# Three v rows of a group added by VectorE, thirteen by TensorE, and a ring of sixteen diagonals

## The chip, the cores and the metric

One core of one Trainium2 chip runs the whole program. The metric is the device time in microseconds. PE is TensorE, DVE VectorE, ACT ScalarE, POOL GpSimd and SP SyncE; each runs its own list of instructions in order, and they wait for one another at semaphores.

## What is computed

An encoder layer over 512 tokens of width 1024: a state-space mixer and latent attention in parallel, a cross-attention to 256 memory tokens, then the expert retrieval with which this document deals, and a last norm. The retrieval, cut to what matters:

```python
def block(xc):                                   # 128 tokens
    q = (xc @ w_q).reshape(T, 8, 2, 128)         # 8 heads, two halves
    s = einsum('thsd,hsnd->thsn', q, sub_keys)
    s1, i1 = top_k(s[:, :, 0], 16);  s2, i2 = top_k(s[:, :, 1], 16)
    cand_s = s1[..., :, None] + s2[..., None, :]
    cand_i = i1[..., :, None] * 128 + i2[..., None, :]
    top_s, pos = top_k(cand_s, 16)
    idx = take_along_axis(cand_i, pos);  gate = softmax(top_s)
    u = take(u_emb, idx, axis=0)                 # rows of 1024 floats
    act = gelu(einsum('thkd,td->thk', u, xc))
    vv = take(v_emb, idx, axis=0)
    return einsum('thk,thkd->td', gate * act, vv)
```

The result is added to the residual stream H, and `rms_norm(H)` is the output. All of it is float32.

## The kernel before

The mixers, the attention and the cross-attention come first; the retrieval begins with the first gather at 767 us. From there the work is cut into 32 groups, numbered g: 8 heads (h), for each the 4 tiles of 128 tokens (t), g = 4h + t. A group needs 16 u rows and 16 v rows for each of its 128 tokens. One gather (line 2003, an indirect DMA that POOL issues) brings one row for each token: 128 rows of 4 KB, so a group has 32 gathers. What each engine does in iteration g:

- POOL (lines 2018 to 2028) issues by turns u row s of group g+1 and v row s of group g, s from 0 to 15. Both have rings of 12 buffers. A u gather waits until the dot product that read its buffer 12 rows ago is done (semaphore `dots`), a v gather until the matmuls that read its buffer 12 rows ago are done (`v_summed`). So v row 12 of group g waits for v row 0 of the same group, and v row 3 of group g for row 7 of group g-1.
- DVE (lines 1473 to 1489) finds the sixteen best keys of group g+2 (`topk`, 25 small steps, each waiting for the one before), takes the finished sum of group g-1 from two PSUM banks into H (`take_sum`, line 1471), makes the 16 dot products of group g+1 (line 1457, one each u row), then, after ACT's gelu, multiplies gelu by gate (`weights`, line 1463, semaphore `w_ready`).
- ACT (lines 943 to 961) copies the queries of head h+1 out of PSUM for t below 2 (line 926), does the exponentials of the gates of group g+2 (930), builds 16 diagonal matrices from the identity and the weights of group g (941), and does the gelu of group g+1 (934). There are 8 diagonal buffers; diagonal s waits until the matmuls of 8 rows ago are done. The gelu stands behind all 16 diagonals in ACT's order.
- PE (lines 1880 to 1885) makes, for t below 2, the queries of head h+1 (line 1854) and the scores from their copy (line 1864), and then sums the group: for each v row, two products of the diagonal with half of the row, 128x512 each, accumulated in two banks (line 1876). The profile has two MATMUL records for each float32 product, so 64 for a group.

After the last group, DVE computes the last norm's variance, ACT its root, and the rows go out.

## Time and profile before

| what | value |
|---|---|
| median of 3 runs | 2350.29 us (2326.3 to 2372.87) |
| the profiled execution | 2343.97 us, span 2342.2 us |
| PE busy | 1807.4 us, 77% |
| DVE busy | 1444.4 us, 62% |
| POOL busy | 1186.4 us, 51% |
| ACT busy | 566.2 us, 24% |
| mean granted clock of PE | 0.896 |
| DMA queue of the gathers | 147840 packets, 537.99 MB, 60.9% of 16 engines' span |

The retrieval takes from 767 us to the end, two thirds of the span. A busy PE there is pipelined matmuls with modelled ends. "Idle before" in the rows below is the time in which the engine did nothing just before such an instruction, with what ended it; "issue" means that the profile shows nothing that it waited for, and "remote" a semaphore whose sender the profile does not name. Every POOL gather has some 0.30 us of idle before it even with nothing to wait for.

### The profile page before, as it was taken

How to read it: one execution, taken by the hardware profiler on the slowest of the kernel's cores; microseconds unless marked ns; L12 is line 12 of the kernel's file. 1: busy time of each engine (PE TensorE's matmuls, PEld its weight loads, DVE VectorE, ACT ScalarE, POOL GpSimd, SP SyncE). 2: the span in 40 equal slices, each digit the busy share in tenths (PEclk: the TensorE clock that was granted, in tenths of full speed). 3: DMA queues.
4: the chain of work that ended last, by engine and by line, in shares of the span. 5: the costliest groups of instructions: out<-in, count | busy, mean ns of one | idle time of the engine just before them, and what ended most of it. 6: DMA issues, size and time to landing. Idle time of an engine off the chain costs nothing.

```text
span 2342.2 us, 19472 instructions
## 1 busy us (share of the span) xinstructions
PE 1807.4 (77%) x6023; PEld 1001.9 (43%) x6023; DVE 1444.4 (62%) x2989; ACT 566.2 (24%) x1201; POOL 1186.4 (51%) x1173
## 2 busy tenths in 40 slices
PE   5978899999998567667777768768857786687587
PEld 5546336779976433223323323323323332232233
DVE  5697773434434566557566676667667666486545
ACT  2344442233333022112111211221211121122111
POOL 6970000000001446765776577667767777667674
PEclk9988999999999778888988889979979898898799
DMA  4303211334323569988999999999999999989997
GB/s 110 63 10 50 68 32 50 95 100 143 126 81 99 190 248 350 367 336 318 387 354 339 343 370 367 379 362 363 382 361 373 365 370 368 346 325 378 349 374 279
DMA packets 243552, 607.27 MB, mean 259 GB/s; under 512 B 38597, under 2 KB 109434, under 8 KB 243450
## 3 DMA queue, kind: packets, MB, share of 16 engines
q0 software_dynamic: 147840, 537.99, 60.9%
q1 hardware_dynamic: 95610, 68.04, 10.4%
q8 instruction: 50, 0.82, 0.1%
q14 instruction: 52, 0.43, 0.1%
HBM read 601.76 MB, written 2.10 MB: 258 GB/s over the span
## 4 chain that ended last, share of the span: by engine, by line
PE 49%; issue 17%; DVE 11%; POOL 9%; another core or an unknown queue 9%; DMA 3%; ACT 2%; SPq 0%; DVEq 0%; ACTq 0%; POOLq 0%
PE bank L1876 26%; PE bank L1565 18%; POOL R L2003 5%; DVE R L991 3%; PE bank L1854 3%; DMA R<-in_peer_v,R 2%; POOL WS L2003 1%; POOL slabs L2003 1%; PE bank L1554 1%; PE bank L1864 1%; DMA XN<-in_x 1%; DVE stat L1249 1%; POOL H L1909 1%; ACT WSr L654 1%
## 5 line engine op out<-in xcount | busy, mean ns | idle before, releaser
L1876 PE MATMUL bank<-R 128*128 128x512 f32 x2048 | 963.9, 629 | 239.4 <-issue 209.4
L1876 PEld LDWEIGHTS bank<-R 128*128 128x128 f32 x2048 | 404.3, 202 | 790.4 <-issue 754.5
L2003 POOL DMA_INDIRECT R<-in_peer_v,R x512 | 525.1, 1026 | 287.7 <-issue 128.8
L941 ACT ACTIVATE R<-cst,R 128x128 f32<-128x128 f32 x512 | 179.7, 393 | 589.4 <-PE bank L1876 327.2
L1999 POOL TENSOR_TENSOR FTr<-slabs,FTr 128x2048 fp32r<-128x2048 f32 x1 | 4.5, 4512 | 542.9 <-ACT FTr L654 542.9
L1457 DVE CUSTOM_DVE_ANT_0 R<-slabs,XN 128x1024 f32<-128x1024 f32 x172 | 210.7, 1225 | 59.8 <-DMA slabs<-in_peer_u,R 33.8
L1457 DVE CUSTOM_DVE_ANT_0 R<-R,XN 128x1024 f32<-128x1024 f32 x168 | 205.7, 1225 | 63.1 <-DMA R<-in_peer_u,R 40.4
L1457 DVE CUSTOM_DVE_ANT_0 R<-WS,XN 128x1024 f32<-128x1024 f32 x172 | 210.7, 1225 | 53.1 <-DMA WS<-in_peer_u,R 32.5
L1565 PE MATMUL bank<-R 128*64 128x64 f32 (+7 forms) x792 | 203.7, 408 | 50.5 <-DVE H L1394 12.8
L2003 POOL DMA_INDIRECT slabs<-in_peer_u,R x172 | 175.1, 1018 | 128.2 <-issue 51.2
L2003 POOL DMA_INDIRECT WS<-in_peer_u,R x172 | 173.3, 1007 | 81.4 <-issue 50.9
L2003 POOL DMA_INDIRECT R<-in_peer_u,R x168 | 169.3, 1008 | 61.7 <-issue 49.7
L1565 PEld LDWEIGHTS bank<-R 128*64 128x64 f32 (+3 forms) x792 | 101.1, 167 | 124.9 <-issue 78.8
L1854 PE MATMUL bank<-FT,slabs 128*128 128x512 f32 (+1 forms) x256 | 118.7, 605 | 31.8 <-issue 25.2
L1864 PE MATMUL bank<-R 128*128 128x128 f32 x120 | 26.5, 390 | 128.1 <-ACT R L926 66.8
L1024 DVE TENSOR_TENSOR WSr<-slabs,WSr 128x1024 fp32r<-128x1024 f32 (+2 forms) x47 | 60.7, 1292 | 103.8 <-ACT WSr L654 103.8
L1471 DVE TENSOR_TENSOR H<-bank,H 128x512 f32<-128x512 f32 x64 | 44.3, 691 | 102.2 <-remote 61.8
L1565 PE MATMUL bank<-Rr,WSr 128*128 128x512 f32 (+1 forms) x448 | 95.4, 366 | 0.0
L991 DVE TENSOR_TENSOR R<-R 128x512 f32<-128x512 f32 (+4 forms) x91 | 76.2, 838 | 27.5 <-POOLq L1987 21.6
L1854 PEld LDWEIGHTS bank<-FT,slabs 128*128 128x128 f32 x256 | 51.8, 205 | 95.5 <-issue 87.7
L926 ACT ACTIVATE R<-bank 128x512 f32<-128x512 f32 (+1 forms) x16 | 9.1, 570 | 319.7 <-remote 286.9
L1565 PEld LDWEIGHTS bank<-Rr,WSr 128*128 128x128 f32 x448 | 77.7, 189 | 13.7
(217 smaller groups left out, 2044.1 us busy)
## 6 DMA issues: line engine op xcount, KB each, us to landing
slabs<-in_w_in SPq DMA_DIRECT2D x17, 512.0 KB, 5.3
slabs<-in_w_mem_kv SPq DMA_DIRECT2D x8, 1024.0 KB, 5.4
slabs<-in_w_peer_q SPq DMA_DIRECT2D x8, 1024.0 KB, 6.7
R<-in_peer_v,R POOLq DMA_INDIRECT x512
slabs<-in_w_in SPq DMA_DIRECT2D x4, 1024.0 KB, 15.0
slabs<-in_w_ssm_glu SPq DMA_DIRECT2D x16, 256.0 KB, 3.1
slabs<-in_w_out SPq DMA_DIRECT2D x4, 1024.0 KB, 5.1
slabs<-in_w_mem_q SPq DMA_DIRECT2D x4, 1024.0 KB, 5.1
```

The lines of the kernel that those rows point to most:

```text
L654: act.activation(hi, src, ACT.Copy).then_inc(w_hi, 1)
L941: act.activation(diag[s % DRING], ident, ACT.Copy, scale=wgt[t % 2][:, s:s + 1]).then_inc(diag_done, 1)
L991: step(dve.tensor_tensor(out, a, b, op))
L1024: dve.tensor_tensor(lo, src, hi, ALU.subtract).then_inc(w_lo, 1)
L1249: step(dve.tensor_reduce(c, b[:, 0:width], AX.X, ALU.max))
L1457: dve.tensor_tensor_reduce(prod, Ub[i % URING], xn[:, t, :], 1.0, 0.0, ALU.mult, ALU.add, act_row[:, s:s + 1]).then_inc(dots, 1)
L1471: lstep(dve.tensor_tensor(h, ps[2 * (t % 2) + n][:, :], h, ALU.add))
L1565: last = pe.matmul(dst, lhs, rhs, start=(n == 0), stop=(n == len(terms) - 1))
L1854: ins = pe.matmul(ps[4 + s][:, cols], qw[:, k, columns(s)], FT[:, k, cols], start=(k == 0), stop=(k == KD - 1))
L1864: ins = pe.matmul(ps[6 + s][:, columns(t)], qhs[s][:, columns(t)], keys, start=True, stop=True)
L1876: last = pe.matmul(ps[2 * (t % 2) + n][:, :], diag[s % DRING], Vb[i % VRING][:, 512 * n:512 * n + 512], start=(s == 0), stop=(s == TOPK - 1))
L2003: pool.indirect_dma_start(out=dst, out_offset=None, in_=table, in_offset=bass.IndirectOffsetOnAxis(ap=ix[:, s:s + 1], axis=0)).then_inc(si ...
```

## The change

- Rows 0, 1 and 2 (`VSLOTS = 3`) of each group leave PE and the diagonals. DVE multiplies each of them by its weight and adds it to H, with one `scalar_tensor_tensor` a row over 128x1024 (`add_rows`), each counted in a new semaphore `v_added`. In DVE's order they stand between the eighth and the ninth dot product.
- A group is 13 rows (`PSLOTS`) for PE and ACT; counts of `diag_done` and `v_summed` are in thirteens.
- A v gather whose buffer held row 0, 1 or 2 waits for `v_added`, the others for `v_summed`.
- There are 16 diagonal buffers; the new eight lie in unused space.
- For t below 2 the scores are issued after the matmuls of v row 8, not ahead of the group.
- In the last group the two roots of ACT stand after all diagonals.

```diff
--- before.py
+++ after.py
@@ -78,7 +78,9 @@
 TOPK_STEPS = 25
 SLAB = 2048
 URING, VRING = 12, 12
-DRING = 8
+VSLOTS = 3
+PSLOTS = TOPK - VSLOTS
+DRING = 16
 
 
 def host_constants():
@@ -311,7 +313,7 @@
         qh2 = reg(0, 2, T)
         SC = reg(1024, NT, 2, NK)
         Vb = [reg(3072 + D * i, D) for i in range(VRING)]
-        diag = [reg(19456 + P * i, P) for i in range(DRING)]
+        diag = [reg((19456 if i < 8 else 1024) + P * i, P) for i in range(DRING)]
         gprow = reg(23040, D)
         gfrow = reg(24064, D)
         prod = reg(25088, D)
@@ -379,6 +381,7 @@
         dots, gelu_done, w_ready, diag_done, v_summed = [
             sem(n) for n in ("dots", "gelu_done", "w_ready", "diag_done", "v_summed")]
         acc_taken, final_done = sem("acc_taken"), sem("final_done")
+        v_added = sem("v_added")
         xg_done = sem("xg_done")
 
 
@@ -933,12 +936,13 @@
                 act.wait_ge(dots, (g + 1) * TOPK)
                 act.activation(gel, act_row, ACT.Gelu_apprx_tanh).then_inc(gelu_done, 1)
 
-            def diagonals(g, t, first=False, slots=range(TOPK)):
+            def diagonals(g, t, slots=range(VSLOTS, TOPK)):
                 act.wait_ge(w_ready, g + 1)
                 for s in slots:
-                    if not first or s >= DRING:
-                        act.wait_ge(v_summed, g * TOPK + (s - DRING + 1))
-                    act.activation(diag[s % DRING], ident, ACT.Copy,
+                    i = g * PSLOTS + s - VSLOTS
+                    if i >= DRING:
+                        act.wait_ge(v_summed, i - DRING + 1)
+                    act.activation(diag[i % DRING], ident, ACT.Copy,
                                    scale=wgt[t % 2][:, s:s + 1]).then_inc(diag_done, 1)
 
             def head(h, first=False, last=False):
@@ -950,12 +954,11 @@
                         gate_exponentials(g + 2)
                     if last and t == NT - 1:
 
-                        diagonals(g, t, slots=range(DRING))
+                        diagonals(g, t)
                         final_root(0)
                         final_root(1)
-                        diagonals(g, t, slots=range(DRING, TOPK))
                     else:
-                        diagonals(g, t, first and t == 0)
+                        diagonals(g, t)
                     if not last or t < NT - 1:
                         gelu_of(g + 1)
 
@@ -1465,11 +1468,20 @@
 
             def take_sum(g, t):
 
-                dve.wait_ge(v_summed, (g + 1) * TOPK)
+                dve.wait_ge(v_summed, (g + 1) * PSLOTS)
                 for n in range(2):
                     h = H[:, t, 512 * n:512 * n + 512]
                     lstep(dve.tensor_tensor(h, ps[2 * (t % 2) + n][:, :], h, ALU.add))
                 dve.sem_inc(acc_taken, 1)
+
+            def add_rows(g, t):
+
+                for s in range(VSLOTS):
+                    i = g * TOPK + s
+                    dve.wait_ge(ld_v[i % VRING], (i // VRING + 1) * 16)
+                    dve.scalar_tensor_tensor(H[:, t, :], Vb[i % VRING], wgt[t % 2][:, s:s + 1], H[:, t, :],
+                                             ALU.mult, ALU.add).then_inc(v_added, 1)
+                    dve.wait_ge(v_added, g * VSLOTS + s + 1)
 
             def head(h, first=False, last=False):
 
@@ -1482,8 +1494,12 @@
                         topk((t + 2) % NT)
                     if not first or t:
                         take_sum(g + (-1), (t - 1) % NT)
-                    if not last or t < NT - 1:
-                        dot_products(g + 1, (t + 1) % NT)
+                    more = not last or t < NT - 1
+                    if more:
+                        dot_products(g + 1, (t + 1) % NT, range(TOPK // 2))
+                    add_rows(g, t)
+                    if more:
+                        dot_products(g + 1, (t + 1) % NT, range(TOPK // 2, TOPK))
                         weights(g + 1, (t + 1) % NT)
                     if ahead:
                         gates_of(g + 2, t)
@@ -1865,24 +1881,27 @@
                 ins.then_inc(s_filled, 1)
 
 
-            def group(g, t, taken=True):
+            def group(g, t, taken=True, then=None):
                 if taken:
                     pe.wait_ge(acc_taken, g - 1)
-                for s in range(TOPK):
+                for s in range(VSLOTS, TOPK):
                     i = g * TOPK + s
+                    n_pe = g * PSLOTS + s - VSLOTS
                     pe.wait_ge(ld_v[i % VRING], (i // VRING + 1) * 16)
-                    pe.wait_ge(diag_done, g * TOPK + (s + 1))
+                    pe.wait_ge(diag_done, n_pe + 1)
                     for n in range(2):
-                        last = pe.matmul(ps[2 * (t % 2) + n][:, :], diag[s % DRING], Vb[i % VRING][:, 512 * n:512 * n + 512],
-                                         start=(s == 0), stop=(s == TOPK - 1))
+                        last = pe.matmul(ps[2 * (t % 2) + n][:, :], diag[n_pe % DRING], Vb[i % VRING][:, 512 * n:512 * n + 512],
+                                         start=(s == VSLOTS), stop=(s == TOPK - 1))
                     last.then_inc(v_summed, 1)
+                    if then and s == TOPK // 2:
+                        scores(*then)
 
             def head(h, first=False, last=False):
                 for t in range(NT):
-                    if t < 2 and not last:
+                    then = (h + 1, t) if t < 2 and not last else None
+                    if then:
                         queries(h + 1, t)
-                        scores(h + 1, t)
-                    group(h * NT + t, t, taken=not first or t >= 2)
+                    group(h * NT + t, t, taken=not first or t >= 2, then=then)
 
             for b in range(8):
                 pe.wait_ge(drained[b], uses[b])
@@ -2012,7 +2031,11 @@
             def v_row(g, t, s):
                 i = g * TOPK + s
                 if i >= VRING:
-                    pool.wait_ge(v_summed, i - (VRING - 1))
+                    was_g, was = divmod(i - VRING, TOPK)
+                    if was < VSLOTS:
+                        pool.wait_ge(v_added, was_g * VSLOTS + was + 1)
+                    else:
+                        pool.wait_ge(v_summed, was_g * PSLOTS + was - VSLOTS + 1)
                 gather(Vb[i % VRING], peer_v, idx[t], s, ld_v[i % VRING])
 
             def head(h, first=False, last=False):
```

POOL's list keeps all gathers in their order; three waits of a group have another semaphore. This is the second half of a group's gathers, before:

```order
L2003 DMA WS<-in_peer_u,R 128x1024 [waits dots]
L2003 DMA R<-in_peer_v,R 128x1024 [waits v_summed]
L2003 DMA WS<-in_peer_u,R 128x1024 [waits dots]
L2003 DMA R<-in_peer_v,R 128x1024 [waits v_summed]
L2003 DMA WS<-in_peer_u,R 128x1024 [waits dots]
L2003 DMA R<-in_peer_v,R 128x1024 [waits v_summed]
L2003 DMA WS<-in_peer_u,R 128x1024 [waits dots]
L2003 DMA R<-in_peer_v,R 128x1024 [waits v_summed]
```

and now (rows 12 to 15 of u and v by turns):

```order
L2022 DMA WS<-in_peer_u,R 128x1024 [waits dots]
L2022 DMA R<-in_peer_v,R 128x1024 [waits v_added]
L2022 DMA WS<-in_peer_u,R 128x1024 [waits dots]
L2022 DMA R<-in_peer_v,R 128x1024 [waits v_added]
L2022 DMA WS<-in_peer_u,R 128x1024 [waits dots]
L2022 DMA R<-in_peer_v,R 128x1024 [waits v_added]
L2022 DMA WS<-in_peer_u,R 128x1024 [waits dots]
L2022 DMA R<-in_peer_v,R 128x1024 [waits v_summed]
```

No gather moved. v rows 12, 13 and 14 of a group now wait for DVE, row 15 for PE.

DVE's list in iteration 9, around the eighth dot product, before (each dot product is a row with a tile and a short row that reads its sum):

```order
L1457 ISA R<-R,XN 128x1024 [waits ld_u10,dots]
L1457 ISA R 128x1
L1457 ISA R<-R,XN 128x1024 [waits ld_u11,dots]
L1457 ISA R 128x1
L1457 ISA R<-slabs,XN 128x1024 [waits ld_u0,dots]
```

and now:

```order
L1460 ISA R<-R,XN 128x1024 [waits ld_u10,dots]
L1460 ISA R 128x1
L1460 ISA R<-R,XN 128x1024 [waits ld_u11,dots]
L1460 ISA R 128x1
L1482 SCALAR_TENSOR_TENSOR H<-R,H 128x1024 [waits ld_v0,dots]
L1482 SCALAR_TENSOR_TENSOR H<-R,H 128x1024 [waits ld_v1,v_added]
L1482 SCALAR_TENSOR_TENSOR H<-R,H 128x1024 [waits ld_v2,v_added]
L1460 ISA R<-slabs,XN 128x1024 [waits ld_u0,v_added]
```

The three adds come behind the u rows that the first eight dot products wait for, and ahead of the other eight.

PE's list over one head, before (x counts products, two for a v row):

```order
L1864 MATMUL bank<-R 128x128 x4
L1876 MATMUL bank<-R 128x512 x96
L1854 MATMUL bank<-FT,slabs 128x512 x8
L1864 MATMUL bank<-R 128x128 x4
L1876 MATMUL bank<-R 128x512 x32
L1854 MATMUL bank<-FT,slabs 128x512 x8
```

and now:

```order
L1870 MATMUL bank<-FT,slabs 128x512 x8
L1893 MATMUL bank<-R 128x512 x12
L1880 MATMUL bank<-R 128x128 x4
L1893 MATMUL bank<-R 128x512 x66
L1870 MATMUL bank<-FT,slabs 128x512 x8
L1893 MATMUL bank<-R 128x512 x12
L1880 MATMUL bank<-R 128x128 x4
L1893 MATMUL bank<-R 128x512 x14
```

A group fell from 32 products to 26, and the scores moved from ahead of it to behind its sixth row.

## Rows read from the trace of the kernel before

**Rows 1.** Stretches: each engine's busy us and count, granted clock, DMA share, GB/s.

```profile
857.00:2332.00 1475.00, 1090.46 (x2376) 468.04 (x2375) 958.27 (x2158) 282.66 (x681) 1001.85 (x984) 0.88 0.94 355
1850.00:1900.00 50.00, 41.39 (x97) 19.11 (x98) 30.43 (x72) 13.46 (x33) 37.29 (x35) 0.87 1.01 387
```

**Rows 2.** Groups of instructions on POOL, 857 to 2332 us: busy, mean ns, idle before.

```profile
L2003 POOL DMA_INDIRECT R<-in_peer_v,R x500 | 512.6, 1025 | 284.0 <-issue 125.1 <-remote 91.1 <-PE bank L1876 67.8
L2003 POOL DMA_INDIRECT WS<-in_peer_u,R x164 | 165.7, 1010 | 79.0 <-issue 48.5 <-DVE R L1457 30.5
L2003 POOL DMA_INDIRECT slabs<-in_peer_u,R x160 | 162.7, 1017 | 54.1 <-issue 48.2 <-DVE R L1457 5.9
L2003 POOL DMA_INDIRECT R<-in_peer_u,R x160 | 160.9, 1006 | 59.3 <-issue 47.2 <-DVE R L1457 12.0
```

**Rows 3.** A wait on POOL, same stretch: us in total, times, longest.

```profile
POOL R L2003 <- remote: 91.1, 49, 4.8
```

**Rows 4.** Groups of instructions on DVE, same stretch, shapes apart.

```profile
L1457 DVE CUSTOM_DVE_ANT_0 R<-WS,XN 128x1024 f32<-128x1024 f32 x168 | 205.8, 1225 | 53.0 <-DMA WS<-in_peer_u,R 32.5 <-DVE R L1457 6.7 <-issue 4.5
L1457 DVE CUSTOM_DVE_ANT_0 R<-slabs,XN 128x1024 f32<-128x1024 f32 x164 | 200.9, 1225 | 59.6 <-DMA slabs<-in_peer_u,R 33.8 <-issue 10.4 <-DVE R L1457 5.0
L1457 DVE CUSTOM_DVE_ANT_0 R<-R,XN 128x1024 f32<-128x1024 f32 x164 | 200.8, 1225 | 63.0 <-DMA R<-in_peer_u,R 40.4 <-issue 6.7 <-DVE R L1457 5.6
...
L1463 DVE TENSOR_TENSOR R<-R 128x16 f32<-128x16 f32 x31 | 5.4, 175 | 69.7 <-issue 46.1 <-ACT R L934 22.5 <-DVE R L1457 1.1
...
L1471 DVE TENSOR_TENSOR H<-bank,H 128x512 f32<-128x512 f32 x62 | 42.9, 691 | 83.6 <-remote 61.8 <-PE bank L1876 12.5 <-DVE R L1444 2.7
...
L1500 DVE SCALAR_TENSOR_TENSOR XN<-H,stat,R 128x1024 f32<-128x1024 f32 x2 | 2.6, 1284 | 0.1
```

**Rows 5.** In order of time, iteration 3: first dot product, u row 12.

```profile
1013.70 1.23 DVE L1457 CUSTOM_DVE_ANT_0 R<-WS,XN 128x1024 f32<-128x1024 f32 x1 [0.19 <-DVE H L1471]
...
1015.20 1.81 POOL L2003 DMA_INDIRECT WS<-in_peer_u,R  x1 [10.63 <-DVE R L1457]
```

**Rows 6.** In order of time, iteration 12: a gather, eighth dot product, v row 12.

```profile
1441.57 0.96 POOL L2003 DMA_INDIRECT R<-in_peer_v,R  x1 [0.30 <-PE bank L1876]
...
1441.75 1.22 DVE L1457 CUSTOM_DVE_ANT_0 R<-R,XN 128x1024 f32<-128x1024 f32 x1
...
1446.63 1.61 POOL L2003 DMA_INDIRECT R<-in_peer_v,R  x1 [0.30 <-issue]
```

**Rows 7.** In order of time, iterations 0 and 30: eighth dot product, v row 12.

```profile
865.75 1.22 DVE L1457 CUSTOM_DVE_ANT_0 R<-R,XN 128x1024 f32<-128x1024 f32 x1
...
866.35 1.45 POOL L2003 DMA_INDIRECT R<-in_peer_v,R  x1 [6.16 <-PE bank L1876]
...
2286.69 0.96 POOL L2003 DMA_INDIRECT R<-in_peer_v,R  x1 [0.30 <-issue]
...
2290.68 1.22 DVE L1457 CUSTOM_DVE_ANT_0 R<-R,XN 128x1024 f32<-128x1024 f32 x1
```

**Rows 8.** POOL in order of time, iteration 8: its v row 12.

```profile
1259.21 1.40 POOL L2003 DMA_INDIRECT R<-in_peer_v,R  x1 [6.21 <-PE bank L1876]
```

**Rows 9.** ACT in order of time, iteration 8: copy, diagonals.

```profile
1252.46 0.60 ACT L926 ACTIVATE R<-bank 128x512 f32<-128x512 f32 x1 [24.05 <-remote]
...
1254.68 2.43 ACT L941 ACTIVATE R<-cst,R 128x128 f32<-128x128 f32 x8
```

**Rows 10.** PE in order of time, iteration 8: scores, then the group.

```profile
1253.11 2.08 PE L1864 MATMUL bank<-R 128*128 128x128 f32 x8 [13.10 <-issue]
1255.21 7.16 PE L1876 MATMUL bank<-R 128*128 128x512 f32 x12
```

**Rows 11.** PE in order of time, one whole group (16).

```profile
1623.34 27.70 PE L1876 MATMUL bank<-R 128*128 128x512 f32 x64 [0.94 <-issue]
```

**Rows 12.** DVE and PE in order of time, the end.

```profile
2302.12 31.12 PE L1876 MATMUL bank<-R 128*128 128x512 f32 x68 [2.36 <-issue]
...
2333.28 1.42 DVE L1471 TENSOR_TENSOR H<-bank,H 128x512 f32<-128x512 f32 x2 [18.59 <-PE bank L1876]
```


## Prediction

> **What bounds the kernel now.** I read the slices of the page first: from a third of the span on, the DMA row stands at 9 while no engine does, and that stretch is the retrieval. So I took the stretch from 857 to 2332 us by itself [rows 1]: POOL busy 1001.85 us for its 984 gathers, DVE 958.27, PE 1090.46 with pipelined records, DMA share 0.94 at 355 GB/s. In its best 50 us the DMA queues moved 387 GB/s at a share of 1.01. A group is 32 gathers of 128 rows of 4 KB, 16.78 MB: 43.4 us at 387 GB/s. The stretch holds 984 / 32 = 30.75 groups, so a group takes 1475 / 30.75 = 48.0 us. The DMA is near its limit, not at it; what is missing are times in which POOL has nothing that it may issue.
>
> POOL is in order, so its list adds up [rows 2]. Busy 1001.85 us, and 0.30 us ahead of each gather even where nothing is waited for, 295 us: 1297 us, or 42.2 a group. The rest is waiting: the v gathers have 284.0 us of idle time ahead of them against 150 for 500 gathers, so 134 are waits for buffers; the u gathers have 79.0 + 54.1 + 59.3 = 192.4 against 145, so 47. "Remote" waits stand only ahead of v gathers, though u and v come by turns; so I read them as `v_summed` that arrived late, like those that name PE. Of these the 49 "remote" ones last 4.8 us at most [rows 3].
>
> DVE is the second loop [rows 4]. A group's 16 dot products have 53.0 + 59.6 + 63.0 = 175.6 us of idle time in all, of which some 0.04 each (20) is normal; 156, or 5.1 a group, is waiting for u rows, so DVE's own round is 48.0 - 5.1 = 42.9 us. In this round stand 69.7 us ahead of `weights` (waiting for the gelu, which stands behind the diagonals) and 83.6 ahead of the take of PE's sum. POOL and DVE are thus both within 6 us of the period, and each waits for the other.
>
> **The change part by part.**
>
> *Adds on DVE.* The nearest instruction is the one of line 1500, the same operation with the same shape: 1.284 us [rows 4], with 0.04 between two as between dot products. Three a group: 4.0 us, 123 us over 30.75 groups. In H and Vb both inputs lie in SBUF, as those of the dot products do, so the v data need nothing more. Below nothing is excluded.
>
> *Where they stand.* u row 12 of the next group may be issued as soon as the first dot product has ended, and POOL does wait for that when DVE is late: in iteration 3 the dot product starts at 1013.70 and POOL has stood for 10.63 us [rows 5]. Now v row 12, POOL's next gather, waits for eight dot products and an add. Take iteration 12: the eighth ends at 1441.75 + 1.22 = 1443.0, the add would be done and seen at 1444.6, and v row 12 was issued at 1446.63 [rows 6]: nothing is lost. In iteration 0 it would be at 865.75 + 1.22 + 1.6 = 868.6 against 866.35, and in iteration 30 at 2293.5 against 2286.69 [rows 7], 6.8 us late. I did this for all 31 iterations: 22 are late, 116 us in sum, the largest 13.2. Two gathers on their way, 43.4 / 32 = 1.36 us each, cover 2.7 us of each, which leaves 62 us. Behind the waiting v row stand u rows 13 to 15, for which DVE waits, and the whole next group.
>
> *Waits that go.* v row 12 waited for PE's first row of the group, as in iteration 8, for 6.21 us [rows 8]; there are nine such waits of over 2 us, 46 us in all, this one the third longest, and they go. The other 88 of the 134 us wait for rows 4 to 15 of the group before. PE now reaches each of these three rows sooner.
>
> *The diagonals and the gelu.* Sixteen buffers for thirteen diagonals: ACT hardly ever waits for PE, and the gelu is free as soon as the dot products are. 69.7 us fall to about 31 x 0.35 = 11: 59 us, or 1.9 a group, off DVE's round. The eight diagonals that are built at once take 2.43 us already [rows 9].
>
> *Scores in mid-group.* They cost 2.08 us of PE, but in iteration 8 they ran from 1253.11 to 1255.19, while ACT went from the copy of the queries at 1252.46 over the exponential to the first diagonals at 1254.68; PE's group starts at 1255.21, a diagonal's 0.4 us after that [rows 9, 10]. So this edit is worth nothing ahead of the group, its cover being ACT; without the cover it would be 2.08 us in 14 groups, 29 us. In mid-group it costs nothing either, while PE isn't the bound.
>
> *PE.* A whole quiet group takes 27.70 us, 0.43 a record, so a v row 1.73 and three rows 5.2 us [rows 11]. That is more than the longest of the 49 waits of [rows 3]. If the signals come by as much sooner, all 88 us go; if they come late for a cause that isn't PE's work, none. Half of the take's 83.6 us should go too, 1.35 us a group: between nothing and 2.7. At the end the last group's 64 records lie bare between 2304 and DVE's take at 2333.28 [rows 12], so there 5.2 us are gained for certain.
>
> *A port rule.* A gather beside a dot product can be as quick as any: 0.96 us at 1441.57, with DVE multiplying from 1441.75 [rows 6]. Over the stretch they average 1.02 [rows 2] against 0.95, so I charge the adds no more than 0.1 us for each of some 90 gathers beside them, 9 us. The Trainium skill (SBUF — State Buffer, Who interferes with whom) says that a VectorE instruction with two SBUF inputs holds off a GpSimd instruction that reads SBUF, the later one fully blocked. If a gather were blocked for each add, 92 x 1.28 = 118 us would be added, by rows and not by a figure of the page; the dot products are such instructions already, and the rows beside them speak against it.
>
> *The sum.* DVE's round becomes 42.9 + 4.0 - 1.9 - 1.35 = 43.6 us where no data is late, POOL's 42.2 plus what it waits. So the period lies between 43.6 and, if the freed time is only waited again at v row 12, 48.0. The shortfall in 22 of 31 iterations says that POOL will wait there often; the 5.1 us that DVE waits for u rows now say that it will arrive earlier when POOL does. I take 46.5, two thirds of the way back: 1.5 x 30.75 = 46 us, and the end's 5, 51. Against this execution's own span 2342.2 that is 2291, and with the 1.8 us around it 2293 to 2294. The execution of these rows, 2343.97, is 6 us under the median of 2350.29, which I leave as noise.
>
> **The rivals.**
>
> *A clear gain, period 43.6.* DVE sets the pace and its round has no more late signals. 4.4 x 30.75 + 5 = 140 us less: 2204. For it: the DMA could do it (43.4). Against it: nothing would be left for jitter between two loops that are chained with no slack.
>
> *Nothing much moves.* The signals that come late are late because the DMA queues are full, not because PE has much to do. A fuller queue then makes as much waiting as was freed. For it: 61.8 us of DVE's waits for PE's sum end "remote" [rows 4], like POOL's. Period 47.5: 15 + 5 less, 2324.
>
> *Slower, through v row 12.* One mechanism: POOL waits for DVE's eight dot products and the add, with none of the 88 us freed. 62 + 9 - 5 = 66 more: 2410. It decides from the point where the waits at v row 12 pass 2 us a group more than what is freed elsewhere. For it: 22 of 31. Against it: the gelu's 1.9 us and the take's bring DVE there sooner, which pays for most of the adds.
>
> *The blocked gathers* of the rule above would end at 2294 + 118 = 2412 as well; I give them 2 in 100, within the 21 of the slower case. That the change does not do what it says I leave out: the order of the instructions shows it.
>
> **How the numbers follow.** Forecast (2260 to 2325) 0.42, clear gain 0.12, nothing much 0.25, slower 0.21. Two per cent, about what a measurement of this kernel can tell from no change, is 2303 and 2397 against the median. Faster: the clear gain, 0.27 of the forecast's 0.42, 0.02 of the third: 0.41. Slower: two thirds of the last, 0.14. The rest 0.45. The range from 2230 to 2390 leaves out most of the clear gain and half of the slower case.
>
> **What would show it.** Right: PE's group at 22 to 23 us in quiet stretches; idle time ahead of `weights` near 11 us in all; adds of 1.28 us, 96 of them; waits of POOL on v gathers that have moved from PE and "remote" to DVE's line of the adds, and are fewer than 134 us; a DMA share over 0.94. Wrong: POOL's waits on the adds over 110 us with "remote" waits as before (slower); a share of 1.0 (clear gain); gathers with a mean well above 1.02 (the port); DVE's small steps stretched further (nothing much).

## The result, and the profile after

The changed kernel takes **2448.66 us**, median of 5 runs (2424.37 to 2490.98), against 2350.29 before (2326.3 to 2372.87): ratio 1.0438, 95% interval 1.0379 to 1.0497. It is slower by over 4%, above the predicted range of 2230 to 2390. The profiled execution is the longest of the five, 42 us above their median and in a slower state than three of them, so its rows show the loss too large, and the main waits are read from variants of the changed kernel as well.

The page of after, and the retrieval's stretch of both kernels (columns as in [rows 1]):

```profile
span 2489.2 us, 18701 instructions
...
PE 1690.8 (68%) x5639; PEld 928.6 (37%) x5639; DVE 1568.1 (63%) x3085; ACT 511.0 (21%) x1105; POOL 1194.8 (48%) x1173
...
q0 software_dynamic: 147840, 537.99, 56.9%
...
DVE 30%; issue 23%; PE 21%; POOL 11%; DMA 7%; another core or an unknown queue 5%; ACT 1%; SPq 1%; DVEq 0%; ACTq 0%; POOLq 0%
...
857.00:2480.00 1623.00, 972.13 (x1988) 392.75 (x1986) 1079.25 (x2253) 227.77 (x585) 1009.46 (x984) 0.81 0.85 323
```

Against [rows 1] POOL is busy for the same 1000 us in 984 gathers, but in 1623 us instead of 1475, and the DMA share fell from 0.94 to 0.85. Nothing became more expensive; POOL stands still for longer. The groups of POOL and its waits, and DVE's lines, in the same stretch of after:

```profile
L2022 POOL DMA_INDIRECT R<-in_peer_v,R x500 | 518.7, 1037 | 363.5 <-DVE H L1482 185.9 <-issue 139.6 <-remote 30.6
L2022 POOL DMA_INDIRECT WS<-in_peer_u,R x164 | 166.8, 1017 | 93.0 <-issue 52.0 <-DVE R L1460 40.9
L2022 POOL DMA_INDIRECT slabs<-in_peer_u,R x160 | 163.4, 1021 | 78.3 <-issue 47.6 <-DVE R L1460 30.8
L2022 POOL DMA_INDIRECT R<-in_peer_u,R x160 | 161.5, 1009 | 84.5 <-issue 46.9 <-DVE R L1460 37.6
...
POOL R L2022 <- DVE H L1482: 185.9, 24, 10.1
POOL R L2022 <- PE bank L1893: 7.4, 13, 2.5
...
L1482 DVE SCALAR_TENSOR_TENSOR H<-R,H 128x1024 f32<-128x1024 f32 x96 | 123.4, 1285 | 7.1 <-DVE R L1460 1.7 <-issue 1.6
L1474 DVE TENSOR_TENSOR H<-bank,H 128x512 f32<-128x512 f32 x63 | 43.6, 692 | 86.4 <-PE bank L1893 32.5 <-remote 23.6 <-DVE R L1447 13.3
L1466 DVE TENSOR_TENSOR R<-R 128x16 f32<-128x16 f32 x31 | 5.4, 175 | 13.6 <-issue 5.8 <-ACT R L937 3.9 <-DVE R L1460 2.1
```

Ahead of the v gathers stand 363.5 us, where [rows 2] had 284.0, and 185.9 of them are 24 waits for an add. The waits on PE fell from 67.8 to 7.4 and the "remote" ones from 91.1 to 30.6. Ahead of the u gathers DVE's dot product now ends 109.3 us of waiting, where [rows 2] had 48.4. So both of POOL's links to DVE grew, by 247 us, and the others lost 121. Two variants that come further below, with shorter profiled executions, show the same waits for an add: 179.2 us in 24 with half rows, 151.4 in 22 with the diagonals first.

One round in order of time. First POOL, whose gathers from 1603.64 to 1632.02 follow one another with no wait:

```profile
1601.06 0.95 POOL L2022 DMA_INDIRECT R<-in_peer_v,R  x1 [0.31 <-remote]
...
1631.07 0.95 POOL L2022 DMA_INDIRECT slabs<-in_peer_u,R  x1 [0.30 <-issue]
1634.47 0.94 POOL L2022 DMA_INDIRECT R<-in_peer_v,R  x1 [2.46 <-PE bank L1893]
1637.34 1.81 POOL L2022 DMA_INDIRECT WS<-in_peer_u,R  x1 [1.93 <-DVE R L1460]
1647.53 1.87 POOL L2022 DMA_INDIRECT R<-in_peer_v,R  x1 [8.38 <-DVE H L1482]
```

Then PE and DVE, same round:

```profile
1606.31 1.98 PE L1893 MATMUL bank<-R 128*128 128x512 f32 x4 [1.19 <-DMA R<-in_peer_v,R]
1618.04 7.29 PE L1893 MATMUL bank<-R 128*128 128x512 f32 x12 [9.74 <-DMA R<-in_peer_v,R]
...
1616.97 0.18 DVE L1447 SCALAR_TENSOR_TENSOR R<-R 128x16 uint32<-128x16 f32 x1
1634.24 1.42 DVE L1474 TENSOR_TENSOR H<-bank,H 128x512 f32<-128x512 f32 x2 [17.09 <-PE bank L1893]
1635.84 1.23 DVE L1460 CUSTOM_DVE_ANT_0 R<-WS,XN 128x1024 f32<-128x1024 f32 x1 [0.19 <-DVE H L1474]
...
1645.98 3.93 DVE L1482 SCALAR_TENSOR_TENSOR H<-R,H 128x1024 f32<-128x1024 f32 x3
```

The two pieces together tell the price. u row 12 (1637.34) had to wait for the first dot product, and v row 12, the very next gather, waited 8.38 us for the add, since eight dot products and an add take from 1635.84 to 1647.3. Of the 24 waits 17 are of 8.38 or 8.39 us: whenever POOL has caught up with DVE at u row 12, it pays the whole of it. Meanwhile the DMA queues run empty (columns as in [rows 1]; the last two are their share and GB/s):

```profile
1640.00:1644.00 4.00, 1.30 (x4) 0.23 (x2) 3.90 (x7) 0.00 (x0) 0.00 (x0) 1.00 0.39 122
1644.00:1648.00 4.00, 0.00 (x0) 0.00 (x0) 3.89 (x6) 0.00 (x0) 0.47 (x1) 0.72 0.00 0
```

The other thing to see is why DVE was late here: it stood for 17.09 us before the take. The take of this group waits for PE's last row of it, and that is the record at 1606.31, ended by 1608.3 (all 32 x 52 records of the groups are in the trace, and by their count the rows from 1618.04 on are the next group's, whose diagonals ACT built at 1614.37). Its signal was seen 26 us later, by DVE at 1634.24 and by POOL at 1634.47 alike. I had read such waits as short ones.

The waits and the key search in both traces. "Loop" is the time from the first dot product of group 1 to the last one; the waits are POOL's beyond 0.30 us a gather; the last column adds up DVE's gaps of over 0.5 us ahead of the small steps of the key search in the loop.

| kernel | loop | at u row 12 | v rows 12 to 14 | other v | key search |
|---|---|---|---|---|---|
| before | 1444 | 45 | 46 | 88 | 132 |
| after | 1592 | 108 | 180 | 34 | 249 |

After's waits at v rows 12 to 14 are +134 us, at u row 12 +63, at the other v rows -54; together 143 of the 148 us of the longer loop.

### The profile page after: what moved, and what is told of

Read it like the earlier page. It is cut to its first block, busy times and chain, and to the rows that moved or that the text cites. A ratio compares the mean times of both kernels' runs of the same rounds, so it can differ in the third digit from the quotient of the medians.

```text
span 2489.2 us, 18701 instructions
## 1 busy us (share of the span) xinstructions
PE 1690.8 (68%) x5639; PEld 928.6 (37%) x5639; DVE 1568.1 (63%) x3085; ACT 511.0 (21%) x1105; POOL 1194.8 (48%) x1173
## 4 chain that ended last, share of the span: by engine, by line
DVE 30%; issue 23%; PE 21%; POOL 11%; DMA 7%; another core or an unknown queue 5%; ACT 1%; SPq 1%; DVEq 0%; ACTq 0%; POOLq 0%
PE bank L1581 18%; POOL R L2022 7%; DVE R L1460 4%; DVE R L994 3%; PE bank L1893 2%; DVE H L1474 2%; DMA WS<-in_peer_u,R 2%; DMA slabs<-in_peer_u,R 2%; DVE H L1482 2%; DVE R L1413 2%; DVE R L1414 2%; DMA R<-in_peer_u,R 2%; DVE R L1415 2%; DVE R L1417 1%
## 5 line engine op out<-in xcount | busy, mean ns | idle before, releaser
L1893 PE MATMUL bank<-R 128*128 128x512 f32 x1664 | 866.8, 671 | 643.7 <-issue 278.5
L1893 PEld LDWEIGHTS bank<-R 128*128 128x128 f32 x1664 | 338.0, 213 | 1161.6 <-issue 808.7
L2022 POOL DMA_INDIRECT R<-in_peer_v,R x512 | 531.2, 1037 | 367.2 <-DVE H L1482 185.9
L937 ACT ACTIVATE R<-R 128x16 f32<-128x16 f32 x32 | 6.9, 216 | 834.7 <-issue 465.4
L1482 DVE SCALAR_TENSOR_TENSOR H<-R,H 128x1024 f32<-128x1024 f32 x96 | 123.4, 1285 | 7.1 <-DVE R L1460 1.7
L1027 DVE TENSOR_TENSOR WSr<-slabs,WSr 128x1024 fp32r<-128x1024 f32 (+2 forms) x47 | 60.7, 1292 | 103.9 <-ACT WSr L657 103.9
L945 ACT ACTIVATE R<-cst,R 128x128 f32<-128x128 f32 x416 | 124.6, 386 | 2.2 <-remote 1.5
L1474 DVE TENSOR_TENSOR H<-bank,H 128x512 f32<-128x512 f32 x64 | 44.3, 692 | 86.4 <-PE bank L1893 32.5
```

The costliest lines, as they stand in the source:

```text
L945: act.activation(diag[i % DRING], ident, ACT.Copy, scale=wgt[t % 2][:, s:s + 1]).then_inc(diag_done, 1)
L1027: dve.tensor_tensor(lo, src, hi, ALU.subtract).then_inc(w_lo, 1)
L1474: lstep(dve.tensor_tensor(h, ps[2 * (t % 2) + n][:, :], h, ALU.add))
L1482: dve.scalar_tensor_tensor(H[:, t, :], Vb[i % VRING], wgt[t % 2][:, s:s + 1], H[:, t, :], ALU.mult, ALU.add).then_inc(v_added, 1)
L1893: last = pe.matmul(ps[2 * (t % 2) + n][:, :], diag[n_pe % DRING], Vb[i % VRING][:, 512 * n:512 * n + 512], start=(s == VSLOTS), stop=(s == ...
L2022: pool.indirect_dma_start(out=dst, out_offset=None, in_=table, in_offset=bass.IndirectOffsetOnAxis(ap=ix[:, s:s + 1], axis=0)).then_inc(si ...
```

## The experiments

Runs of one group shared a core and its runs of the kernel before. All ratios are to these.

**First group: the parts one by one** (before 2349.08 us). Theory O at this point: the order, POOL waiting at v row 12 for DVE's middle, costs the time. Rival L: DVE's load of 4 us an iteration does.

The wait alone, in the kernel before:

```diff
                 if i >= VRING:
                     pool.wait_ge(v_summed, i - (VRING - 1))
+                if s == 12 and g + 1 < NG:
+                    pool.wait_ge(dots, (g + 1) * TOPK + 9)
                 gather(Vb[i % VRING], peer_v, idx[t], s, ld_v[i % VRING])
```

> The kernel before, in which v row 12 of each group also waits for the ninth dot product of the next group, about the moment at which the first add would be done. No add is made. Theory O (the order: POOL's list stands still at v row 12 while the DMA queues run dry): most of the 98 us come back, 2420 to 2450 us, with waits of some 8 us at that gather. Theory L (load: the 4.0 us of adds in each of DVE's rounds make the time): under 2370 us.

Measured: 2418.39, ratio 1.0268 (1.0207 to 1.0329), just under the range of theory O. POOL's waits at v rows 12 to 14 are 135 us (before 46), those at the other v rows fell from 88 to 29, and POOL's gathers themselves took 38 us more in the loop (1026 against 988), which no edit here explains:

```profile
L2003 POOL DMA_INDIRECT R<-in_peer_v,R x500 | 537.4, 1075 | 314.1 <-issue 136.0 <-DVE R L1457 77.9 <-PE bank L1876 76.9
```

The load alone, in the kernel before, is three operations of the same form into a scratch tile, between the eighth and ninth dot product:

```diff
-                        dot_products(g + 1, (t + 1) % NT)
+                        dot_products(g + 1, (t + 1) % NT, range(TOPK // 2))
+                        for s in range(3):
+                            lstep(dve.scalar_tensor_tensor(prod, xn[:, (t + 1) % NT, :], wgt[t % 2][:, s:s + 1],
+                                                           xn[:, (t + 1) % NT, :], ALU.mult, ALU.add))
+                        dot_products(g + 1, (t + 1) % NT, range(TOPK // 2, TOPK))
```

> The kernel before, in which DVE makes three operations of the adds' form and shape (into a scratch tile, so they change no result) between the eighth and the ninth dot product of each iteration but the last. PE still sums all sixteen rows. Theory O: 31 x 4.0 = 124 us of DVE work hide mostly behind waiting for u rows, 2350 to 2385 us. Theory L: 2420 us or more.

Measured: 2346.33, ratio 1.0016 (0.9963 to 1.0069). The load costs nothing there that can be told from zero. L falls.

The changed kernel with `VSLOTS = 0`, so that ring, scores and split remain:

> The changed kernel with no row on DVE (VSLOTS = 0): what is left is the ring of sixteen diagonals and the scores in mid-group. Both theories: the idle time ahead of the weights falls from 70 us to about 11, so 2300 to 2345 us. If it is over 2380 us, the loss is in the diagonals or the scores, and both theories fall.

Measured: 2339.07, ratio 0.9943 (0.9904 to 0.9981). The wait for the gelu went as predicted (its line has 11.3 us of idle time ahead, where [rows 4] had 69.7), but ahead of the take the idle time rose (these rows hold all 64 instructions of the take, the last group's too, for which before has 102.2 us and not the 83.6 of [rows 4] with 62):

```profile
L1474 DVE TENSOR_TENSOR H<-bank,H 128x512 f32<-128x512 f32 x64 | 44.2, 691 | 124.0 <-remote 60.5 <-PE bank L1893 55.8 <-issue 2.0
L1466 DVE TENSOR_TENSOR R<-R 128x16 f32<-128x16 f32 x31 | 5.4, 176 | 11.3 <-issue 6.0 <-ACT R L937 3.9 <-DVE R L1460 1.4
```

So of the 58 us freed at the gelu 22 came back as waiting for PE's sum, and the gain is 0.6%.

The changed kernel with `add_rows` ahead of all dot products, so that v row 12 waits for DVE's first work after the take:

> The changed kernel with the three adds ahead of all sixteen dot products. v rows 12 to 14 are then free before u row 12 is, so POOL's one wait is that for the first dot product, 4.0 us later than before. Theory O: 2330 to 2390 us, and no wait of some 8 us at v row 12. Theory L: as the changed kernel, 2430 to 2460 us.

Measured: 2508.88, ratio 1.0664 (1.0594 to 1.0733), a clear miss. POOL's waits at v rows 12 to 14 went to zero, and those at u row 12 to 280 us:

```profile
POOL slabs L2020 <- DVE R L1460: 108.2, 10, 21.9
POOL WS L2020 <- DVE R L1460: 104.7, 9, 21.3
POOL R L2020 <- DVE R L1460: 96.9, 8, 14.8
```

The order of the adds is thus not the point. Whatever stands ahead of a dot product for which POOL waits is paid, and DVE was later than before by more than the adds: its key search had 419 us of gaps.

**Second group: without a wait for the adds** (before 2326.88). Theory C: POOL's wait for the chain take, first dot product, later ones is what is paid, and load ahead of the first dot product costs too. Rows 4, 5 and 6 instead of 0, 1 and 2 on DVE; their buffers are wanted again only by v rows 0, 1 and 2 of the next group, so POOL has no wait for the adds in mid-group (the start of the edit):

```diff
-VSLOTS = 3
+VSLOTS, VLO = 3, 4
+ON_PE = [s for s in range(TOPK) if not VLO <= s < VLO + VSLOTS]
```

> The changed kernel with rows 4, 5 and 6 of each group on DVE in place of 0, 1 and 2; the adds stand where they stood, behind the eighth dot product. The buffers that they free are wanted by v rows 0 to 2 of the next group, some 9 us after v row 12. v row 12 waits for PE's first row again. Theory O (POOL's wait at v row 12 in mid-group is the loss, DVE's adds themselves are free there): 2310 to 2360 us, like the kernel with no adds. If the loss is the coupling of POOL to DVE's adds wherever it is: 2400 us or more.

Measured: 2423.36, ratio 1.0348 (1.0257 to 1.0438). POOL waits 10 us at v rows 12 to 14 and 222 at u row 12. Another miss: taking the wait away moved it. What also grew is DVE's key search, 372 us of gaps against 132. Why POOL should wait so much longer for the first dot product here than with the load alone, whose DVE work has the same place (222 us against 80), no run tells. One such stretch of this kernel, POOL and DVE:

```profile
2004.20 0.95 POOL L2025 DMA_INDIRECT R<-in_peer_v,R  x1 [0.30 <-issue]
...
1991.56 0.09 DVE L1418 MATCH_VALUE_LOAD R<-R 128x8 f32 x1 [1.09 <-DVE R L1417]
1993.67 0.29 DVE L1419 MAX8 R<-R 128x8 f32<-128x128 f32 x1 [1.76 <-issue]
1995.06 0.09 DVE L1420 MATCH_VALUE_LOAD R<-R 128x8 f32 x1 [1.09 <-issue]
1997.86 0.18 DVE L1435 CAST R<-R 128x32 f32<-128x32 uint32 x1 [2.44 <-remote]
1999.27 0.42 DVE L1436 TENSOR_TENSOR R<-R 128x256 f32<-128x256 f32 x1 [1.23 <-issue]
2000.66 0.43 DVE L1416 MAX8 R<-R 128x8 f32<-128x256 f32 x1 [0.97 <-DVE R L1436]
2002.06 0.09 DVE L1417 MATCH_VALUE_LOAD R<-R 128x8 f32 x1 [0.97 <-DVE R L1416]
2004.16 0.09 DVE L1418 MATCH_VALUE_LOAD R<-R 128x8 f32 x1 [1.60 <-issue]
2006.96 0.43 DVE L1419 MAX8 R<-R 128x8 f32<-128x256 f32 x1 [2.31 <-remote]
...
2009.87 0.17 DVE L1442 TENSOR_SCALAR R<-R 128x16 uint32<-128x16 uint32 x1 [0.66 <-DVE R L1440]
```

Each step waits for nothing but the one before on DVE itself, and starts 1.40, 2.10 or 2.80 us after it, multiples of 0.70; in after's round above most of the same steps start within 0.04 us of the end of the one before. PE stood idle here from 1982.4 to 2010.65. The last late step starts at 2009.87, some 5 us after POOL's last gather, which ended at 2005.15.

The three extra operations in the kernel before, ahead of all dot products:

> The kernel before, in which DVE makes three operations of the adds' form and shape into a scratch tile ahead of its sixteen dot products, not amid them. No row leaves PE, no v buffer waits for DVE. The kernel with the adds first took 2509 us. Theory C (what sets the time is DVE's chain from its small steps to the first dot product, for which u row 12 and so POOL waits; time amid the dot products is free): 2450 to 2520 us. If the adds' position costs only through v buffers: 2350 to 2380 us.

Measured: 2436.67, ratio 1.0499 (1.0447 to 1.0552), though DVE's load is that of the kernel that lost nothing. The 3.9 us an iteration stand between the take and the first dot product: 31 x 3.9 = 121 us, of which 110 arrive.

Theory S is that full DMA queues stretch DVE's small steps. Half gathers, of 64 partitions, after the first twelve (the other partitions keep old rows, so the sums are not the layer's):

> The kernel before with the same half gathers (output not the reference's). Theory S: the time from the weights to the take falls from 18 us to 12 to 14, PE's late signals go (no diagonal waits much over 1.3 us for a row), 2080 to 2200 us, and the changed kernel with half gathers is within 2 per cent of it. If the changed kernel stays 4 per cent behind, its loss doesn't need full queues.

> The changed kernel with only 64 of 128 rows in each gather after the first twelve u and v gathers; the other partitions keep what is there, so the output is not the reference's. POOL has as many gathers, the DMA queues half the bytes. Theory S (DVE's small steps stretch, from about 12 to over 20 us a group, because the DMA queues are full beside them): the time from the weights to the take falls to 12 to 14 us, and the kernel to 2100 to 2250 us, with a few us of wait at v row 12 left. If the stretching has another cause, it stays at 20 us or more.

Measured: 2326.16, ratio 0.9995 (0.9957 to 1.0032), and 2357.55 from two runs (2338.89 and 2376.22), too few for an interval. I can't use them as meant: the bytes halved (275.84 MB), but the queues stayed busy for 51.8% of the span; a packet took longer. As far as two runs go, the changed kernel lies 31 us, 1.3%, behind here and not 4.4%, although it waits 106 us at v rows 12 to 14 (29 without the change): at u row 12 it waits 18 us and not 92. So a wait at v row 12 isn't lost in every case; why this pair loses less is open.

**Third group: a shorter chain in the key search** (before 2339.65). Theory R: signals travel late, so each of the 25 small steps that waits for the one before costs. The ten steps of the first stage run on two halves by turns, each waiting for the last but one:

```diff
-                for s in range(2):
-                    top16(SC[:, t, s, :], sc1, tv[:, s, :], ti[:, s, :])
+                for k in range(5):
+                    for s in range(2):
+                        ...
+                        lstep([lambda: dve.max(v[:, 0:8], vals),
...
+                               lambda: dve.max_index(ix[:, 8:16], v[:, 8:16], spare)][k](), lag)
```

> The kernel before with its key search in pairs: the five steps on the one half of the keys and the five on the other by turns, each waiting only for its own predecessor, and two more steps that don't wait for the one before. Same instructions, ten fewer waits in a row. Theory R (the stretched time of DVE's small steps is the round trip of each step's own semaphore, at the place that sets the first dot product): 4 to 6 us a group less from the weights to the take, and 2260 to 2320 us. If the steps are late for another reason, the time stays within 1 per cent of before.

> The changed kernel without adds (ring of sixteen, scores in mid-group) and the search in pairs. Theory R: the shortest round of DVE of all four, and so the fastest: 2230 to 2300 us, which would beat both kernels. If R is wrong, about 2339 us as without pairs.

> The changed kernel with the same search in pairs. Theory R: its period is DVE's round, so nearly the whole gain arrives: 31 x 4 to 6 us, 2270 to 2350 us. Otherwise 2430 us or more.

> Rows 4, 5 and 6 on DVE, and the search in pairs. Theory R: DVE's round of 52 us falls to 46 to 48, so 2260 to 2320 us. If R is wrong, 2400 us or more.

Measured, in this order: 2338.61, ratio 1.0002 (0.996 to 1.0043); 2334.96, 0.9957 (0.991 to 1.0003); 2418.19, 1.0282 (1.0197 to 1.0367); 2389.8, 1.0179 (1.0088 to 1.0271). On before and on the kernel without adds it gives nothing; on after 1.0438 becomes 1.0282 and on rows 4 to 6 1.0348 becomes 1.0179, each against its own core's before. That speaks for DVE's round as what sets the pace in the kernels with adds and not in before. It doesn't show it: the intervals of after's pair all but touch (from 1.0379 and to 1.0367), those of rows 4 to 6 overlap (from 1.0257 and to 1.0271), and neither pair stood on one core. The expected times (2270 to 2350 and 2260 to 2320 us) were missed by far.

**Fourth group: full queues, or not?** (before 2326.12). A rival to POOL's issuing as the cause of the late signals was that the DMA queues are full. Half rows on all 128 partitions, after the first twelve gathers (the right halves keep old data):

> The kernel before with gathers of 128 rows of 2 KB (half a row) after the first twelve u and v gathers; the right halves keep old data, so the output is not the reference's. Theory S (late updates need full queues): the key search is not stretched (12 to 14 us from the weights to the take), PE's signals come in time, and the time is 2100 to 2230 us. If the lateness comes from the gathers' count and not from their bytes: as before within 2 per cent, with the key search at 18 us or more.

> The changed kernel with the same gathers of half rows (output not the reference's). Theory S: 2130 to 2280 us, the key search not stretched, v row 12's wait still there. Otherwise: 2380 us or more.

Measured: 2299.28, ratio 0.9844 (0.9767 to 0.9922), and 2414.17 from two runs. The traffic of the first in the stretch:

```profile
857.00:2290.00 1433.00, 1079.66 (x2351) 464.70 (x2349) 951.41 (x2149) 276.23 (x667) 994.04 (x982) 0.88 0.64 185
...
q0 software_dynamic: 83840, 275.84, 41.5%
```

The queues are busy 0.64 of the time instead of 0.94, at half the GB/s, and the key search still has 145 us of gaps (before 132), POOL's waits at other v rows are 84 (88). So the lateness doesn't need full queues. And with half the bytes after loses as much, 2414 against 2299, with 172 us of waits at v rows 12 to 14. Its key search has 108 us of gaps, fewer than the 145 of the kernel before with half rows: the loss doesn't need a key search more stretched than before's.

The diagonals ahead of the exponentials in ACT's order, so that PE starts without waiting for the key search:

> The changed kernel without adds (ring of sixteen, scores in mid-group), with ACT building a group's diagonals ahead of the exponential of the gates of two groups later. PE may then start a group when its weights are ready, some 20 us sooner. Theory P (PE's late start, tied to DVE's key search, makes POOL's waits ahead of v rows, 134 us in the kernel before): 2220 to 2300 us, and most of these waits gone. If POOL's waits move to the u rows instead: 2320 to 2345 us.

> The changed kernel with its adds, diagonals first. Its waits at v row 12 are for DVE's adds and not for PE. Theory O: they stay, some 8 us each, and the time stays at 2400 to 2450 us. If PE's late start had a part in the loss: under 2390 us.

Measured: the kernel without adds 2330.37, ratio 1.0024 (0.998 to 1.0069), the changed one 2427.6, 1.0343 (1.0239 to 1.0446). Ahead of the take the idle time fell to 64.3 us in the first, from 124.0 in the kernel without adds of the first group, and the kernel was no faster: POOL's waits at u row 12 became 105 us instead of 54, those at v rows 12 to 14 fell from 50 to 8. An earlier PE is not worth anything here.

**Fifth group, on another chip** (before **2170.24**, 2168.25 to 2171.75 in 13 runs). The kernel before itself runs 7% faster there. Two kernels ran: wait and load together in the kernel before (here the wait is for eight dot products, some 1.3 us sooner than for the nine of the wait alone), and rows 4 to 6 with a pause of eight small operations on POOL, ahead of u row 6 in each iteration:

> The kernel before with both: v row 12 waits for the eighth dot product of the next group (1.3 us sooner than the add), and DVE makes three operations of the adds' form into a scratch tile behind that dot product. Sixteen rows on PE, eight diagonals, the scores ahead of the group. If the change is these two and nothing else: 2420 to 2460 us, the changed kernel's loss. If the two only add up as measured alone (2.7 and 0 per cent): 2385 to 2405 us.

> The kernel with rows 4, 5 and 6 on DVE (2423 us, 3.5 per cent behind), in which POOL makes eight fills of an unused tile, some 5 us, ahead of u row 6 of each group, that is in the midst of the gathers that run beside DVE's key search. Theory U (an unbroken run of gathers makes DVE's updates late): the search gets shorter by more than a little (rest of DVE's round under 24 us, now 25.7) and the time is the same or up to 2 per cent less, 2340 to 2420 us. If the lateness has nothing to do with the run: POOL's spare time takes the pause at best and the time is the same or more, with the same search.

Measured: wait and load 2169.89, ratio **0.9999** (0.9989 to 1.0008); the pause 2340.72, 1.0773 (1.0745 to 1.08). Their rows, the first three of wait and load, the last of the pause:

```profile
857.00:2100.00 1243.00, 1010.08 (x2223) 412.74 (x2221) 1028.02 (x2180) 267.33 (x638) 948.68 (x944) 0.95 1.02 404
...
L2007 POOL DMA_INDIRECT R<-in_peer_v,R x497 | 495.4, 997 | 158.3 <-issue 133.5 <-PE bank L1880 19.9 <-DVE R L1457 4.9
...
L1471 DVE TENSOR_TENSOR H<-bank,H 128x512 f32<-128x512 f32 x64 | 44.2, 691 | 27.0 <-PE bank L1880 21.3 <-DVE R L1444 0.5
```

```profile
L2054 POOL MEMSET R<- 128x600 f32 x248 | 148.9, 601 | 12.6
```

No "remote" wait, no gap of over 0.5 us in the key search of the loop (132 us in before on its chip), a DMA share of 1.02 at 404 GB/s. POOL issues nearly without a stop: its 497 v gathers have 158.3 us of idle time ahead, 9 more than 0.30 each. Nearly the same wait that cost 2.7% by itself costs nothing here even with the load: POOL waits 17 us at v rows 12 to 14 and 11 at u row 12. The pause, 161 us of POOL's time, arrives as 170 against before: POOL is the bound, its gathers (1004 us), their 0.30 each (291) and the pause add up to 1456 of the loop's 1459. Both kernels were made for a core where signals are late, and neither expectation could be decided as it was written; the changed kernel itself has not run on this chip.

**The kernels side by side**, by the profiled execution of each; columns as in the table above, with the mean of a v gather in ns. That of after is the one of 2490.98 us.

| kernel | loop | at u row 12 | v rows 12 to 14 | other v | key search | v gather |
|---|---|---|---|---|---|---|
| before | 1444 | 45 | 46 | 88 | 132 | 1026 |
| wait alone | 1514 | 49 | 135 | 29 | 111 | 1074 |
| load alone | 1461 | 80 | 19 | 104 | 234 | 1004 |
| load first | 1501 | 184 | 4 | 76 | 310 | 983 |
| after | 1592 | 108 | 180 | 34 | 249 | 1037 |
| no adds | 1462 | 54 | 50 | 83 | 166 | 1038 |
| adds first | 1582 | 280 | 0 | 72 | 419 | 973 |
| rows 4 to 6 | 1529 | 222 | 10 | 54 | 372 | 981 |
| before, half rows | 1405 | 37 | 30 | 84 | 145 | 1039 |
| after, half rows | 1501 | 21 | 172 | 23 | 108 | 1060 |
| before, 64 partitions | 1437 | 92 | 29 | 91 | 273 | 974 |
| after, 64 partitions | 1447 | 18 | 106 | 50 | 55 | 1045 |
| no adds, diagonals first | 1436 | 105 | 8 | 80 | 276 | 1003 |
| wait and load, fast chip | 1292 | 11 | 17 | 2 | 0 | 999 |

The loop grows with the sum of POOL's waits, to which the length of its gathers adds. It does not go with the gaps in the key search: load alone, before with 64 partitions and no adds with diagonals first have 234 to 276 us of them, and their medians are within 0.3% of before's. The gaps are mostly long where POOL waits at u row 12 and shorter where it waits at v row 12; which of the two makes the other, no run tells.

**What the traces say of the signals.** A trace records when a semaphore was updated. For the counter that PE raises once a row, in after's round above:

```
rows' records end    1608.3 | three by 1625.3, then 1628.6, 1631.1, 1633.7      | 1636.3  1638.8
updates (us)         1608.78 1610.92 1615.88 | 1634.21 1637.05 .11 .16 .22 .28 .34 | 1637.97 1638.83
```

For 18 us there is none, then one, then six at 0.06 us distance. Counted back from the last two, which come with their rows, the six are the rows that end from 1621.8 to 1633.7, and the one at 1634.21 is the last row of the group before, of 1608.3; the three ahead of the pause are for rows still earlier. The ends of PE's records are modelled, but where a signal is in time they agree with it (1638.81 and 1638.83). And what is late is the update's own record; DVE and POOL go on within 0.3 us of it. On the fast chip the counter has a record for each of its 512 updates, and none in such a burst. On the others some are missing (392 of 512 in before, 301 of 416 in after), so a row's own delay can only be bounded. In before there are 22 bursts of three or more, in after 9, and each of the 31 lies in a pause of POOL's issuing (1.3 to 10.1 us long), 1.0 to 5.0 us after its last gather. Part of that is by construction, since POOL's pause is often a wait for just this counter. But with the key search above, which loosens some 5 us after POOL's last gather, it makes one picture: where POOL has issued without a pause for some 20 to 28 us (in some rounds over 60), signals of the other engines begin to come late, and they come through when it stops. That is an observation of coincidence. On the fast chip POOL issues for up to 168 us without a pause of 1 us, and nothing is late. Why it happens on four of the chips and the first one, and not on the last, no run tells. One rival stands untested: update records are missing just where signals are late, and all executions here were recorded, so the recording itself may have a part.

## Why the prediction was wrong, point by point

**What bounds the kernel.** POOL 42.2 us a group without waits held: where signals are on time the loop is 1292 us, 41.7 a group. DVE's "own round" of 42.9 us did not. It was the period less its waits for u rows, so it contained the 132 us of stretched key search and the late take as if they were work. On the fast chip DVE waits some 4.9 us a group for u rows, so its round there is 36.8 us with the load of 3.9 in it. The period itself was also read too long: the 1475 us of [rows 1] hold the last group's matmuls, in which nothing is gathered, and the loop's 1444 us over 31 groups give 46.6 us, not 48.0. I had the rows: in [rows 4] 61.8 us before the take end "remote".

**Adds on DVE.** 1.285 us each, 96 of them, as predicted. By themselves they cost nothing amid the dot products (1.0016) and nearly all their length ahead of the first (1.0499).

**Where they stand.** This is the failing step: the shortfall of DVE's middle against v row 12, priced at 62 us. I took before's times of the eighth dot product as fixed and found 116 us of shortfall in 22 iterations, 62 after a cover of 2.7 us each. Measured were 24 waits with 185.9 us, 8.38 the typical one. Two errors: a shortfall is not fixed, since POOL, in 20 of the 24 cases, has already waited for DVE at u row 12, and then pays eight dot products and an add in full; and the cover of 2.7 us is too little for a wait of 8.38, in which the DMA share falls to 0.00 as shown above. The wait alone measured 2.7%, 63 us by 2349. That this is the forecast's 62 is luck: its waits at v rows 12 to 14 rose by 89 us, those at u row 12 by 4, those at the other v rows fell by 59, and its gathers took 38 more.

**Waits that go.** They went: 159 us of waits on PE and "remote" became 38. No time came with them. Even in the wait alone, where PE sums all sixteen rows, the other v rows' waits fell as far (29 us), so this is no effect of PE's shorter group: POOL, held at one place, waits less at the next. The same holds for the gelu: predicted 11 us, measured 13.6, and 11.3 in the kernel without adds, where over a third of what was freed was waited again at the take. Half of the take's 83.6 us should have gone; over the same 62 instructions it has 73.9 (the 86.4 above has the end's 12.48 in it).

**Scores in mid-group.** Worth nothing ahead of the group, as said; in mid-group they ran in 1.05 us. No run has this edit alone.

**PE.** Predicted 22 to 23 us for a quiet group. No whole group was quiet. The best parts are 10.54 us for six rows in one group and 12.18 for seven in another:

```profile
1934.37 10.54 PE L1893 MATMUL bank<-R 128*128 128x512 f32 x24 [2.78 <-ACT R L945]
...
1122.40 12.18 PE L1893 MATMUL bank<-R 128*128 128x512 f32 x28
```

That would make 22.7, but whole groups took 25.2 or more, with the granted clock at 0.81 over the stretch where [rows 1] had 0.88. The end's "certain" 5.2 us did not come either. From `weights` to the take were 30.9 us before; after:

```profile
2448.43 0.17 DVE L1466 TENSOR_TENSOR R<-R 128x16 f32<-128x16 f32 x1 [0.35 <-ACT R L937]
...
2457.34 22.56 PE L1893 MATMUL bank<-R 128*128 128x512 f32 x48 [2.26 <-DMA R<-in_peer_v,R]
2479.94 1.42 DVE L1474 TENSOR_TENSOR H<-bank,H 128x512 f32<-128x512 f32 x2 [12.48 <-PE bank L1893]
```

31.5 us: twelve rows took 22.56, but PE had 2.26 us to wait for a v row and had only come to the group at 2453.

**The port rule.** With 96 adds the gathers' mean rose from 1.025 to 1.037 for v and from 1.010 to 1.017 for the u rows into WS, and their busy time in the stretch by 8.5 us in all. That this is what I had charged (9) is luck: with no added VectorE work the wait alone has 1.074, and with the same 96 adds, placed first, the mean is 0.973. Nothing was held off by a whole add, and these gathers show no price of the adds at all. The Trainium skill (SBUF — State Buffer, Who interferes with whom) states its rule for GpSimd instructions that read SBUF; no row says whether a gather is one, and the 118 us that I had worked out for that case did not come.

**The sum.** "Two thirds of the way back" had no row behind it. The sum put DVE's round at 43.6; in the loops of the table above a group takes 1592 / 31 = 51.4 us in after and 46.6 in before. The nearest rival, "slower, through v row 12", named the mechanism and the decisive point (waits at v row 12 passing 2 us a group more than what is freed), at 2410 us and with a chance of 0.21. Its price was 39 us too small, as the shortfall in it was. Of the sign that I had named for it half came: waits on the adds over 110 us, but the "remote" waits fell from 91.1 to 30.6. "Nothing much moves" had a true half, signals late for a cause that isn't PE's work, and a wrong cause, full queues.

**What is settled and what is open.** Shown: the wait at v row 12 costs 2.7% by itself on a core with late signals; a wait that ends 1.3 us sooner costs, together with the load, nothing on a core without them; the load costs by its place; ring, scores and gelu are worth 0.6% together; moving the wait off v row 12 moves it to u row 12. Argued only: that longer unbroken issuing by POOL makes the key search longer. That a longer key search then feeds the loss is not borne out: after with half rows loses as much without it. Open: why DVE is so late at the first dot product with rows 4 to 6, the 1.7 points between the wait alone and the whole change (1.0268 and 1.0438, not on one core), what makes signals late, and whether the changed kernel loses anything on the fast chip. No version with whole gathers clearly beats before; the kernel without adds comes to 0.9943.

## What to carry to other kernels

When a change ties an engine that feeds the DMA to a point in the middle of another engine's round, price it by the length of the work up to that point, not by the shortfall that today's times show: where the engine has already waited for the first step of that work, it pays the whole of the rest. Before an engine's "own round" is taken as work, look whether its small dependent steps follow one another at once; idle time between steps that wait for nothing but each other isn't work, it changes with the neighbours and can't be spent. And load put on an engine was here free or nearly fully paid by its place: amid operations that nobody waits for (1.0016), or ahead of the first that somebody does (1.0499).

## What the runs showed of the hardware that I had not expected

- The same kernel took 2170.24 us on one chip and 2326 to 2350 on the others, and on the first its runs lie within 0.2%, on the others within 2.5%. A small difference measured on one chip may not be there on another.
- Where signals are late, steps that wait for their own engine's last one mostly start 1.40, 2.10 or 2.80 us apart (rows 4 to 6), and held updates of a counter arrive 0.06 us apart (after); PE's last row of a group was seen up to 26 us after its record's end. The Trainium skill (Perfetto Trace Analysis, Per-engine timelines) says that the propagation of a semaphore lies outside what the profiler reports for an instruction; the rows here agree that such time exists, up to 26 us in after, most of it ahead of the update's own record.
- Half the bytes by half rows on 128 partitions left the queues busy 41.5% of the span instead of 60.9; by whole rows on 64 partitions, in as many packets (83840), 51.8%.
- Indirect gathers issued by GpSimd showed no price of VectorE operations of 1.285 us with both inputs in SBUF: the mean v gather was 1.037 us with 96 of them amid the dot products, 0.973 with 96 ahead of them, and 1.026 and 1.074 in two kernels with none.
